# Reordered loads at the outset, two-pass layer norms, earlier projections and filler matmuls in a two-block model kernel

## The reference

```
h = x                                         # 256 x 1024
for layer in (0, 1):
    mix = mamba2(h) if layer == 0 else diff_attention(h)
    h = layer_norm(ALPHA * h + mix, g_mix, b_mix)          # m0, m1
    h = layer_norm(ALPHA * h + hier_moe(h), g_ffn, b_ffn)  # f0, f1
# second block: 16 meta tokens ahead of the 256
h = h + even_layer(rms_norm(h))               # two attentions side by side
h = h + odd_layer(rms_norm(h))                # gated recurrence

def layer_norm(x, g, b):
    return (x - mean(x)) * rsqrt(var(x) + 1e-5) * g + b
```

## Time and profile before

| | |
|---|---|
| median of 3 runs | 2153.27 us (2151.74 to 2154.38) |
| the profiled execution | 2153.49 us, of it 2151.6 us from first to last instruction |
| TensorE busy | 2006.7 us, 93% |
| VectorE, ScalarE, GpSimd busy | 671.1, 460.2, 57.5 us |
| DMA | 520.06 MB read from HBM, 242 GB/s over the span |
| granted TensorE clock, mean | 0.960 |

### The profile page before, as it was taken

How to read it: one execution, slowest core, us unless ns; L and a number is a source line. 1 busy time by engine, 2 the same in 40 slices (tenths; PEclk the granted TensorE clock), 3 DMA queues, 4 the chain that set the end, 5 groups by cost and what they waited for, 6 DMA issues and landing times.

```text
span 2151.6 us, 20121 instructions
## 1 busy us (share of the span) xinstructions
PE 2006.7 (93%) x8225; PEld 1061.6 (49%) x8225; DVE 671.1 (31%) x1475; ACT 460.2 (21%) x979; POOL 57.5 (3%) x55
## 2 busy tenths in 40 slices
PE   6999989999999997986999999999579999989999
PEld 6888743333333333443333333333245556437874
DVE  2555431111111112223111111111324555424994
ACT  1222211111001101232111101110223423204770
POOL 0000000000000000000000000000000100001110
PEclk9999988999999998987899999999779999999999
DMA  8323346999999958113699999995311122131412
GB/s 349 118 113 118 118 156 258 424 428 425 428 428 428 428 250 326 59 65 156 256 424 425 428 428 427 428 428 252 160 70 70 52 105 105 68 124 57 195 47 91
DMA packets 38269, 522.44 MB, mean 243 GB/s; under 512 B 4368, under 2 KB 4880, under 8 KB 6304
## 3 DMA queue, kind: packets, MB, share of 16 engines
q1 hardware_dynamic: 36880, 515.59, 58.0%
q10 hardware_dynamic: 1296, 5.54, 0.7%
HBM read 520.06 MB, written 1.05 MB: 242 GB/s over the span
## 4 chain that ended last, share of the span: by engine, by line
PE 88%; DVE 7%; ACT 3%; issue 1%; POOL 1%; DMA 0%; SPq 0%; DVEq 0%; ACTq 0%
PE ps L194 33%; PE ps L587 20%; PE ps L609 10%; PE ps L559 6%; PE ps L619 5%; PE ps L574 1%; PE ps L1120 1%; PE ps L991 1%; PE ps L959 1%; PE ps L943 1%; PE ps L846 1%; POOL small L2155 1%; PE ps L964 1%; PE ps L500 1%; PE ps L595 1%
## 5 line engine op out<-in xcount | busy, mean ns | idle before, releaser
L587 PE MATMUL ps<-ring,work 128*64 128x512 f32 x2048 | 445.0, 592 | 0.7 <-issue 0.7
L194 PE MATMUL ps<-xT,ring 128*128 128x272 f32 (+1 forms) x1280 | 300.7, 394 | 0.3 <-DVE xT L1909 0.3
L587 PEld LDWEIGHTS ps<-ring,work 128*64 128x64 f32 x2048 | 148.7, 137 | 290.3 <-issue 290.3
L194 PEld LDWEIGHTS ps<-xT,ring 128*128 128x128 f32 x1280 | 246.0, 194 | 46.9 <-issue 2.5
L609 PE MATMUL ps<-ring,work 128*64 128x512 f32 x1024 | 226.8, 595 | 1.4 <-ACT work L1296 1.4
L194 PE MATMUL ps<-ring,xT 128*128 128x256 f32 (+2 forms) x672 | 209.3, 471 | 1.6 <-DVE xT L1909 1.6
L194 PE MATMUL ps<-ring,big 128*128 128x512 f32 x448 | 201.4, 607 | 4.3 <-ACT ring L1532 1.9
L1779 DVE TENSOR_TENSOR work<-work,ps 128x512 f32<-128x512 f32 x32 | 22.0, 688 | 523.9 <-PE ps L587 523.9
L194 PEld LDWEIGHTS ps<-ring,xT 128*128 128x128 f32 x672 | 128.9, 194 | 78.0 <-issue 65.9
L194 PEld LDWEIGHTS ps<-ring,big 128*128 128x128 f32 x448 | 85.6, 194 | 111.5 <-issue 109.1
L609 PEld LDWEIGHTS ps<-ring,work 128*64 128x64 f32 x1024 | 70.7, 137 | 134.8 <-issue 127.9
(11 more groups left out here) (325 smaller groups left out, 1811.8 us busy)
## 6 DMA issues: line engine op xcount, KB each, us to landing
ring<-in_wg SPq DMA_DIRECT2D x64, 2048.0 KB, 13.8
ring<-in_wu SPq DMA_DIRECT2D x64, 2048.0 KB, 16.8
ring<-in_wd SPq DMA_DIRECT2D x64, 2048.0 KB, 12.4
ring<-in_w_xz SPq DMA_DIRECT2D x8, 2048.0 KB, 16.1
ring<-in_w_odd SPq DMA_DIRECT2D x8, 2048.0 KB, 8.3
ring<-in_w_qkv SPq DMA_DIRECT2D x6, 2048.0 KB, 19.9
ring<-in_w_bc SPq DMA_DIRECT2D x4, 2048.0 KB, 12.4
ring<-in_ssm_out SPq DMA_DIRECT2D x4, 2048.0 KB, 8.3
```

The lines of the kernel that those rows point to most:

```text
L194: i = e.matmul(bout, lhs(k), rhs(k), start=start and k == ks[0], stop=stop and k == ks[-1])
L587: last = e.matmul(b[64 * j:64 * j + 64, :], xgT[:, p % 2, k, 64 * j:64 * j + 64], w[j][:, k, :], start=k == 0, stop=k == 7)
```

## The change

- Outset: `x`, the first weights and the other loads of SyncE come in the order of their use; ScalarE issues four constant loads itself; waits are for single groups (`x_in`, `ident_in`, `first_in`, `consts`, `late`). The first weight slot is loaded in two halves. VectorE copies half of the transposes. TensorE begins four of the six projection parts around the `dt` matmuls instead of after them.
- Layer norm: `(h - mean) * g` and then `h * rs + b`, both on VectorE with `scalar_tensor_tensor`; ScalarE has no part in it any more.
- `tensor_warm` and loops over `ones`: matmuls whose results nobody reads, put where TensorE waits.
- MoE: S is built for a pair before SW, with a signal of its own (`weighted`); the last spread does tile 0 first and signals it (`half_mm`).
- Attention: tile 0's q projection comes before tile 1's transposes; then k and v of tile 0, then tile 1. The `lam` matmul comes after the projections.

```diff
-        xT_in = Sig(sem("xT_in"), turned.keys)
+        xT_in = Sig(sem("xT_in"), [k for k in turned.keys if k[0] != "x0" or k[2] == 0])
...
+        def tensor_warm(e, bank, n):
+
+            for i in range(n):
+                e.matmul(bank[:, :], identb, negU.rearrange("p a b -> p (a b)"), start=True, stop=True)
...
             for t in range(2):
+                if t:
+                    tensor_warm(e, idle, 12)
                 for n in range(2):
                     e.wait_ge(*ln_out(s, t, n))
                     tensor_turn(e, s, t, n, turn[n])
...
             last.then_inc(*lg_mm.up(l))
+            tensor_warm(e, idle, 20)
...
             if p:
                 e.wait_ge(*silu_in(l, p - 1))
+            e.wait_ge(*weighted(l, p))
             b = moe_bank(p - 1, SWTB)
...
-            for n in range(2):
-                for t in range(2):
+            for t in range(2):
+                for n in range(2):
                     last = e.matmul(macc[t][n][:, :], SWT[:, p % 2, t, :], ys[:, n * 512:(n + 1) * 512],
                                     start=p == 0, stop=p == NE // 2 - 1)
-            last.then_inc(*spr_mm.up(l, p))
+                if p == NE // 2 - 1:
+                    last.then_inc(*spr_mm.up(l, p) if t else half_mm.up(l))
+            if p < NE // 2 - 1:
+                last.then_inc(*spr_mm.up(l, p))
...
             e.matmul(b[:, 32:64], triS, mk[:, 1, :], start=False, stop=True).then_inc(*rank_mm.up(l))
+            tensor_warm(e, ps[2], 6)
             tensor_gather(e, l, 0)
...
-            e.wait_ge(consts, 144)
-            e.wait_ge(*zeroed("meta"))
+            e.wait_ge(*zeroed("ones"))
+            for i in range(10):
+                e.matmul(ps[6][:, 0:128], ones[:, :], ones[:, :], start=True, stop=True)
+            e.wait_ge(x_in, 16)
+            e.wait_ge(ident_in, 16)
             for t in range(2):
                 for n in range(2):
                     tensor_turn(e, "x0", t, n, ps[2 * t + n])
...
+            for i in range(8):
+                e.matmul(ps[6][:, 0:128], ones[:, :], ones[:, :], start=True, stop=True)
...
-        def scalar_ln(e, s, t):
-            e.wait_ge(*ln_nm(s, t))
-            for n in range(2):
-                hh = h[:, t, n * 512:(n + 1) * 512]
-                e.activation(hh, hh, ACT.Identity, bias=nm[:, t:t + 1],
-                             scale=rs_[:, t:t + 1]).then_inc(*ln_id.up(s, t, n))
...
         def scalar(e):
-            e.wait_ge(consts, 144)
+            e.dma_start(cF[:, :, :], A["cF"]).then_inc(ident_in, 16)
+            e.dma_start(col[:, :], A["col"]).then_inc(consts, 16)
+            e.dma_start(row[:, :], A["row"].broadcast_to([128, NROW])).then_inc(consts, 16)
+            e.dma_start(cB[:, :, :].bitcast(U16), A["cB"]).then_inc(consts, 16)
...
             e.tensor_scalar(rs_[:, t:t + 1], mv[:, t, 1:2], EPS1, None, ALU.add).then_inc(*ln_var.up(s, t))
+            e.wait_ge(ln_in, load)
+            half = (slice(0, 512), slice(512, 1024))
+            for c_ in half:
+                e.scalar_tensor_tensor(out=h[:, t, c_], in0=h[:, t, c_], scalar=mv[:, t, 0:1], in1=lnb[:, 0, c_],
+                                       op0=ALU.subtract, op1=ALU.mult).then_inc(*vs.up())
+            e.wait_ge(*vs())
             e.wait_ge(*ln_rs(s, t))
...
+            for n, c_ in enumerate(half):
+                e.scalar_tensor_tensor(out=h[:, t, c_], in0=h[:, t, c_], scalar=rs_[:, t:t + 1], in1=lnb[:, 1, c_],
+                                       op0=ALU.mult, op1=ALU.add).then_inc(*ln_out.up(s, t, n))
...
-            e.wait_ge(*spr_mm(l, NE // 2 - 1))
             for t in range(2):
-                vector_residual(e, macc, t, lambda t, n: spr_mm(l, NE // 2 - 1),
+                vector_residual(e, macc, t, lambda t, n: spr_mm(l, NE // 2 - 1) if t else half_mm(l),
                                 moe_res.up(l) if t else None)
...
         def sync(e):
-            e.dma_start(h[:, 0:2, :], A["x"].rearrange("a (t p) d -> p (a t) d", p=128)).then_inc(consts, 16)
...
+            e.dma_start(h[:, 0:2, :], A["x"].rearrange("a (t p) d -> p (a t) d", p=128)).then_inc(x_in, 16)
+            for half, done in ((1, (first_in, 16)), (0, ring("w", 0))):
+                c = slice(256 * half, 256 * half + 256)
+                e.dma_start(kview(8, 512)(ring.view("w", 0))[:, :, c], A["w_xz0"][half]
+                            .rearrange("p (k n) -> p k n", k=8)).then_inc(done[0], 16)
+                if half:
+                    e.dma_start(wdt.rearrange("p k n -> p (k n)"), A["wdt"]).then_inc(consts, 16)
+                    sync_load(e, A["w_bc"][0], "BC", 0)
```

More of the change, by code:

```diff
@@ L456, in tensor_in @@
                 if j == 0:
[L457 removed]
+                    e.wait_ge(*(ring("BC", g // 2) if half else ring("w", g) if g else (first_in, 16)))
                     if g:
@@ L809, in tensor_attention @@
                     e.wait_ge(*ln_out("f0", t, n))
-                    tensor_turn(e, "f0", t, n, ps[2 * t + n])
+                    tensor_turn(e, "f0", t, n, ps[4 * t + n])
+                if t == 0:
+                    e.wait_ge(*xT_in("f0", 0, 1))
+                    tensor_qkv(e, 0, 0, 0)
+            tensor_qkv(e, 0, 1, 0)
+            tensor_qkv(e, 0, 2, 0)
+            e.wait_ge(*xT_in("f0", 1, 1))
+            for w in range(3):
+                tensor_qkv(e, 0, w, 1)
             e.wait_ge(*lp_in(0))
@@ L813, in tensor_attention @@
             ab.gone[id(ps[7])] = lam_e(0)
-            e.wait_ge(*xT_in("f0", 1, 1))
-            for w in range(3):
-                for t in range(2):
-                    tensor_qkv(e, 0, w, t)
             tensor_turn_qk(e, 0, 0)
@@ L1163, in tensor @@
             e.matmul(ps[5][:, 64:96], ones[:, :], dtA[:, 0, :], start=True, stop=True).then_inc(*acum_mm.up(0))
-            for part in range(6):
-                tensor_in(e, 0, part)
+            tensor_in(e, 0, 4)
+            tensor_in(e, 0, 5)
             for g in range(8):
@@ L1180, in tensor @@
             banks = []
-            for what in ("lg", "turn0", "turn1"):
+            for what in ("lg", "turn0", "turn1", "idle"):
                 b, gone = ab.take((what,), routed(1))
@@ L1220, in scalar_mamba @@
             for t in range(2):
-                for n in range(2):
-                    scalar_turned(e, "x0", t, n, ps[2 * t + n])
-            scalar_load_ln(e, 0)
+                scalar_turned(e, "x0", t, 0, ps[2 * t])
+            e.wait_ge(consts, 64)
+            e.activation(nega, R("a_log"), ACT.Exp).then_inc(*nega_e.up(0))
             e.wait_ge(*dt_abs(0))
@@ L1304, in scalar_moe, with scalar_qkv @@
             crowded(e, l, scalar_crowded, x_act, X_ACT, x_go_act)
-        def scalar_qkv(e, hg, w):
-            for t in range(2):
-                e.wait_ge(*qkv_mm(hg, w, t))
-                e.copy((qs, ks_, vs_[hg])[w][:, t, :], ab["qkv", hg, w, t][:, :]).then_inc(*qkv_in.up(hg, w, t))
+        def scalar_qkv(e, hg, w, t):
+            e.wait_ge(*qkv_mm(hg, w, t))
+            e.copy((qs, ks_, vs_[hg])[w][:, t, :], ab["qkv", hg, w, t][:, :]).then_inc(*qkv_in.up(hg, w, t))
         def scalar_turned_qk(e, hg, w):
@@ L1329, in scalar_attention @@
         def scalar_attention(e):
-            for t in range(2):
-                scalar_ln(e, "f0", t)
-                for n in range(2):
-                    scalar_turned(e, "f0", t, n, ps[2 * t + n])
+            for n in range(2):
+                scalar_turned(e, "f0", 0, n, ps[n])
+            scalar_qkv(e, 0, 0, 0)
+            for n in range(2):
+                scalar_turned(e, "f0", 1, n, ps[4 + n])
             e.wait_ge(*ln_out("f0", 1, 1))
@@ L1582, in vector_mamba @@
         def vector_mamba(e):
+            for t in range(2):
+                e.wait_ge(*turned("x0", t, 1))
+                e.tensor_copy(xT[:, 4:8, t * 128:(t + 1) * 128],
+                              ps[2 * t + 1][:, :].rearrange("p (k t) -> p k t", k=4)).then_inc(*xT_v.up(t))
+            e.wait_ge(consts, 64)
+            vector_conv(e, 0, 0)
             e.wait_ge(*dt_mm(0))
@@ L2352, in host_layout @@
     D["wdt"] = rows(w, (6144, 6176))
-    D["w_xz"] = np.stack([rows(w, (256 * g, 256 * g + 256), (2048 + 256 * g, 2304 + 256 * g)) for g in range(8)])
+    D["w_xz0"] = np.stack([rows(w, (0, 256)), rows(w, (2048, 2304))])
+    D["w_xz"] = np.stack([rows(w, (256 * g, 256 * g + 256), (2048 + 256 * g, 2304 + 256 * g)) for g in range(1, 8)])
     D["w_bc"] = np.stack([rows(w, (4096 + 256 * g, 4352 + 256 * g), (5120 + 256 * g, 5376 + 256 * g)) for g in range(4)])
```

112 lines of the change are left out of this document (54 added, 58 removed).

## The result

Before: median 2152.79 us (2151.74 to 2154.38, 4 runs). Changed: median **2105.8 us** (2103.74 to 2106.1, 4 runs). The ratio is 0.9779, with an interval of 0.9762 to 0.9796. The profiled execution took 2105.5 us with a span of 2103.7.

What follows compares the result with a forecast made beforehand. TensorE, busy 93% of the span, was taken as the bound, with gains only where it stands or runs slowly. Gains 11 + 6.2 + 6.2 + 6.7 + 6.8 = 36.9 from 2153.5 gave 2116.6 us; range 2108 to 2128.

Steps and rivals of the forecast that it cites:

- The pair loop: MoE pairs: TensorE sets the loop, so the 32 pairs were taken as unchanged and shifted as a block.
- the outset: Start of the kernel up to the first scan: 11 us won, taken between 13.5 and 8.0.
- m1: Second layer's MoE router: same waits as the first layer's, so 6.2 us won.
- f0: Ahead of attention: 6.7 us won, bound by the q weights' landing, with 1.6 back for the `lam` exponential; 8.3 if hidden.
- f1: Last cross-attention part: 6.8 us won, 1.24 from the residual, 1.8 from tile 0's norm, 3.7 at tile 1.
- a fast and a slow case: Outset: if fillers bring the fast pace, scan at 38.3 and 13.5 us won; if not, 43.8 and 8.0.
- The first half of the weights is no bound: Outset: 3 MB must have landed before the projection parts begin, which at 423 GB/s from 2.5 on is 10.
- m0: First layer's MoE router: 6.2 us won, including 2.5 by the end of router matmuls and 2.2 in the gather.
- The outset that stays slow: Rival: no fast pace from matmuls on `ones`, 8 won at the outset, about 2121; within 2109 to 2126, together 0.80.
- Overrun of the router's fillers: Rival: the clock drops, 20 fillers take 8.5 us against a 5.5 wait, both routers give -2 each: 2133; chance 0.13.
- The greater gain: Rival: fast pace also through first projections ahead of attention and in the last part, `lam` hides: 2107 or less; 0.05.
- The pair loop didn't lengthen: Rival: MoE pairs get longer through the `weighted` wait or DMA; 1.15 us a pair would eat the gains; chance 0.02.

Runs made afterwards that it cites:

- Experiment 12: The kernel before with only 9 fillers ahead of the second pair's gather in each MoE: 2148.4 us, ratio 0.998.
- experiments 7 and 8: The kernel before with S built before SW alone: 2141.9 us; the kernel before with the 12, 20 and 6 router fillers alone: 2139.3 us.
- experiment 3: The changed kernel with the lists S and SW built in turns as before: 2109.7 us, ratio 0.9805.
- the repeats: The kernel before run twice more with nothing changed: 2145.9 and 2148.4 us.
- the repeat: The changed kernel run once more with nothing changed: 2106.6 us.
- experiment 2: The changed kernel without the 10 and 8 matmuls on ones at the outset: 2108.6 us, ratio 0.9805.
- Experiment 4: The changed kernel with the layer norm of before, over VectorE, GpSimd and ScalarE: 2113.4 us, ratio 0.9827.
- 5: The changed kernel with both tiles transposed ahead of the first q projection: 2108.2 us, ratio 0.9798.
- 6: The changed kernel with more fillers, 24 and 8 ahead of attention, 52 and 12 in the last part: 2099.1 us, ratio 0.9753.
- experiment 10: The changed kernel with fillers 17 and 8 ahead of attention, 41 and 12 in the last part, 19 behind each head group: 2089.5 us; again 2088.1 and 2091.0.

## Why the prediction was too high

**The step that failed.** "The pair loop is set by TensorE there and the change adds nothing to it, so I take the 32 pairs as unchanged and shift them as a block." That was read from a stretch in the middle of the loop, 393 to 423 us, and it holds for every pair but the second of each layer. There VectorE has just begun to make lists and TensorE stands for it; the new list order makes the wait 1.50 in place of 2.39 (0.9 us), and the clock doesn't fall behind it (1.7 us). Twice 2.6 is 5.2 us, nearly half of the 11.0 missed (47.9 less 36.9). The prediction costed the list order at the first gather only, and the row of TensorE's waits for L1740, four times, not two, shows this one too. Experiment 12 shows that the 1.7 is the standing itself. Either edit of the change can save it: the list order alone did in both layers, the router fillers alone in one of two (experiments 7 and 8), and with the fillers in, mixed lists cost only the 0.9 (experiment 3). Over all profiles the gather behind a wait of 2.4 us was slow 6 times of 6 in the kernel before and 1 time of 4 in kernels with router fillers, and behind 1.5 us in none of 24.

**The other term put at nothing** is attention, 4.0 for 0 (below): the sum was worked from one profile of before, and that one had a slow stretch which is no part of the code. The rest, 2.0 at the outset, 0.8 in m1 and -1.1 in f0, f1 and the rest together, makes up the 11.0 within rounding. With the outset's 2.0 and the second pairs' 5.2 alone the time would have been 2109.4, inside the range.

**The outset**, 13.0 for 11. The sum took the middle between a fast and a slow case, because "TensorE was busy 10.7 of the 11.6 us from 11.22 to 22.86 and stayed slow". That was one execution: the repeats reached the fast pace within the same 32 matmuls. The branch with the fast pace, 13.5 with the scan at 38.3, was the right one: 38.85 here and 37.12 in the repeat. The Trainium skill (TensorE: Matmul & The Clock Gate, Part 1: The HAM clock gate) had said it, that sustained activity releases the clock; experiment 2 agrees, 7.1 with fillers in every profile against 10.06 without. Without fillers the pace also rose, only later. Inside the branch three steps were wrong. "The first half of the weights is no bound" was: they were waited for 1.77 us. In this execution the clock fell once more in the third group of 32 matmuls (8.84 for 7.14). And the end was too dear: from the fourth part to the scan the prediction had 9.0, on a path over VectorE and ScalarE, and both profiles have 7.4 (31.44 to 38.85, 29.71 to 37.12). Of the 2.6 from Silu's start to the scan in the earlier trace rows, Silu took only 1.06; the rest was TensorE ending its z parts, on which the scan's transposes follow without idle time. They do so in the changed kernel too, where Silu ends 0.1 us earlier. That 1.6 too much and the dip's 1.7 too little nearly cancel, so the closeness of 38.85 to 38.3 is luck. Read over the profiles of both kernels, the outset is worth 9.6 (48.40 to 38.85) to 14.7 us (51.84 to 37.12).

**m0**, 6.2 for 6.2 in the first profile, each part as reckoned (in the repeat 4.5, see the rivals): tile 1's transposes at 297.61 + 13.0 = 310.6 on the old clock (310.8 predicted), router matmuls 1.98, gather 3.70 for 3.4. The 12 fillers do end late: VectorE finished the norm's second pass, 1.41 us for both halves, at 296.85, so half 0 was there at 296.2 and the transposes began 1.4 us later. Fewer were not tried. **m1** gave 7.0, because before it had been 30.39 against m0's 29.65, at the same code; after, both took 23.4.

**f0**, 6.6 for 6.7. The weights for q bound it as predicted (wait 2.28; 815.6 on the old clock for 815.7), and the path behind them ended at 860.0, to a tenth as reckoned. The exponential of `lam` then costs what was predicted too: 1.7 us for 1.6, as 4.54 against 2.84 in every profile of either order. It does not lie hidden. It only falls behind the start of line 761, so a distance that ends there reads 8.3. Experiment 4 confirms that the norm there is free, and 5 that interleaving the two tiles is worth about 2.6.

**f1**, 6.2 for 6.8: 3.0 up to tile 0's transpose as reckoned, of which experiment 4 gives 1.7 to the norm and so leaves 1.3 for the earlier residual, which no run took alone; 3.35 for 3.7 at tile 1's.

**Attention** behind that, 4.0 for 0 (132.2 to 128.2 us from the first score matmul on). Its code is the same there. Of the 4.0, 3.1 lie in the first 22 us, and this is where the stage scatters. The first profile of before:

```profile
871.20 0.32 PE L755 MATMUL ps<-cB 128*128 128x384 bf16 x1 [0.93 <-ACT ring L1314]
...
877.66 15.12 PE L194 MATMUL ps<-ring,xT 128*128 128x512 f32 x32
892.62 0.49 PE L767 MATMUL ps<-cF,work 128*128 128x128 f32 x3
```

and the second, at the same place:

```profile
867.11 0.32 PE L755 MATMUL ps<-cB 128*128 128x384 bf16 x1 [0.93 <-ACT ring L1314]
...
871.57 14.00 PE L194 MATMUL ps<-ring,xT 128*128 128x512 f32 x32
885.41 0.49 PE L767 MATMUL ps<-cF,work 128*128 128x128 f32 x3
```

The one takes 21.4 us from its first row to its last, the other 18.3. In five of the eighteen profiles it is 21.4 or 21.5 (the first of before, experiments 3, 6 and 12, the first of 10), with a granted clock of 0.66 over the first 10 us, and in the thirteen others 18.3, with 1.00. Counted from line 742 or 761 the whole stage, without the fillers of experiment 10, took 131.5 or 131.6 in the old order and 132.7 to 133.2 in the new one where this dip is absent, and 134.2 to 136.8 where it is present. So the change itself costs attention the wait for `lam` and gains nothing there; the forecast was worked from a profile with the dip (2153.5; single runs reach down to 2145.6). What sets the dip off in a single execution stays open: the wait ahead of it is 0.93 us with it and without it.

**The rivals.** The outset that stays slow did not come: the projections ran at 7.1 us for 32 from their start in all ten profiles with fillers and projections ahead of `dt`. Overrun of the router's fillers cost 1.4 us with the clock up. In the repeat of the changed kernel, where the clock fell to 0.63 from 293 to 297 us, they took 4.22 in place of 2.76 and m0 gave 1.7 less, which is the mechanism of that rival at a fraction of its price. The 12 fillers took 4.2 to 4.5 us in 5 of the 11 profiles of the changed kernel and its variants that have them. The greater gain, "2107 or less", came true by another mechanism than the one it named: f0's and f1's first projections stayed partly slow until experiments 6 and 10 filled their waits, and `lam` did not hide. The pair loop didn't lengthen.

## What to carry to other kernels

A term of zero for a loop wants its first two or three passes read by themselves, since they wait for what the loop later has in stock. Price a wait of TensorE by what runs behind it too: a filled wait of 2.4 us gave back 1.7 us although it stayed as long. End a stage's measure behind everything that the edit moves: f0's, ended at line 761, would make the wait for `lam` look free. And where a stage scatters between executions, read a second profile of the same kernel before a difference is put down to an edit, and look for the one place where the two part. Size fillers by when the awaited work is done, since they cost what they overrun.

## What the runs showed of the hardware

- The 32 `dt` matmuls of 32 columns took 7.04, 5.41 and 4.31 us in three executions of one kernel, and 3.65 to 3.94 behind 32 projection matmuls.
- At the outset the granted clock reads 1.00 both where work runs at the slow and at the fast pace: 5 to 12 us reads 1.00 in the first profile of the changed kernel, whose transposes took 1.97, and in its repeat, where they took 3.68. There the durations tell the pace, not that row.
- In 4 of 10 profiles with the changed outset and its fillers the projections behind the `dt` matmuls fell to the slow pace for a while (8.6 to 8.8 us for 7.15), though TensorE had not stood since 12.1 us; the granted clock of 23 to 28 us was 0.66 in one of them and 1.00 in the repeat without it. All four had waited about 1.7 us ahead of 12.1, but so had three of the six without the dip. No run tells why.
- In 5 of 18 profiles the granted clock fell to 0.66 at the head of attention, behind a wait of 0.93 us in the old order that in other executions of the same kernel cost nothing.
